# Moving the queries of three expert blocks and the attention units in the order of a decoder step

## The reference

```
q = (xt @ w_pq).reshape(PEER_BLOCK, PEER_HEADS, 2, D_HALF)
s = jnp.einsum('thcd,hckd->thck', q, sub_keys).astype(jnp.float32)
s1, i1 = lax.top_k(s[:, :, 0], PEER_TOPK)
s2, i2 = lax.top_k(s[:, :, 1], PEER_TOPK)
...
top, sel = lax.top_k(cand, PEER_TOPK)
idx = jnp.take_along_axis(cidx, sel, axis=-1)
gate = jax.nn.softmax(top, axis=-1)
h = jnp.einsum('td,thkd->thk', xt, u_tab[idx]).astype(jnp.float32)
a = (jax.nn.gelu(h, approximate=False) * gate).astype(xt.dtype)
return jnp.einsum('thk,thkd->td', a, v_tab[idx])
```

## Time and profile before

| | us |
|---|---|
| median of 3 runs | 1735.94 |
| lowest and highest | 1732.04, 1736.52 |
| the profiled execution, its own time | 1738.4 |
| its span, first to last instruction | 1736.6 |
| PE, DVE, ACT, POOL busy | 1307.0, 1171.6, 811.9, 665.7 |
| DMA queue of the gathers | 604.28 MB, 84.8% of the span of 16 engines |

### The profile page before, as it was taken

How to read it: one execution, slowest core, us unless ns; L and a number is a source line. 1 busy time by engine, 2 the same in 40 slices (tenths; PEclk the granted TensorE clock), 3 DMA queues, 4 the chain that set the end, 5 groups by cost and what they waited for, 6 DMA issues and landing times.

```text
span 1736.6 us, 21554 instructions
## 1 busy us (share of the span) xinstructions
PE 1307.0 (75%) x7059; PEld 474.1 (27%) x7059; DVE 1171.6 (67%) x2760; ACT 811.9 (47%) x2335; POOL 665.7 (38%) x583
## 2 busy tenths in 40 slices
PE   7999977797887876667787677777777676766765
PEld 3454532343443321213232111112111111111110
DVE  2444567788667677777776677777766677677664
ACT  1433355776344455445554455455444445444433
POOL 0000134345444444343435454444444444444441
PEclk9999988898999988988878877877888888888866
DMA  9424599999999999999999999999999999999995
GB/s 358 154 108 154 222 351 402 357 397 377 421 421 421 419 395 420 399 405 399 402 393 379 423 421 421 421 422 421 421 420 421 420 416 422 422 421 420 421 421 209
DMA packets 97745, 656.30 MB, mean 378 GB/s; under 512 B 12432, under 2 KB 17168, under 8 KB 20816
## 3 DMA queue, kind: packets, MB, share of 16 engines
q0 software_dynamic: 83056, 604.28, 84.8%
q1 hardware_dynamic: 14576, 50.64, 7.7%
HBM read 651.66 MB, written 4.19 MB: 378 GB/s over the span
## 4 chain that ended last, share of the span: by engine, by line
DMA 44%; PE 25%; DVE 12%; ACT 10%; issue 7%; POOL 1%; ACTq 0%; SPq 0%; DVEq 0%; POOLq 0%
DMA R<-in_peer_uv,R 43%; PE ps L1933 9%; PE ps L1478 6%; DVE R L1416 4%; PE ps L1737 3%; PE ps L1455 2%; ACT L881 2%; ACT R L890 2%; ACT R L885 1%; ACT R L881 1%; ACT L797 1%; PE ps L1463 1%; DVE R L1246 1%; DVE R L1249 1%; DVE R L1247 1%
## 5 line engine op out<-in xcount | busy, mean ns | idle before, releaser
L1933 PE MATMUL ps<-R 64*64 64x512 f32 x4608 | 751.4, 734 | 394.5 <-ACT R L890 393.2
L612 POOL DMA_INDIRECT R<-in_peer_uv,R x576 | 663.7, 1152 | 973.3 <-PE ps L1933 767.6
L1416 DVE CUSTOM_DVE_ANT_0 R<-R 128x1024 f32<-128x1024 f32 x576 | 700.1, 1224 | 392.1 <-DMA R<-in_peer_uv,R 388.0
L881 ACT ACTIVATE R<-R 128x1 f32<-128x1 f32 x576 | 115.9, 201 | 616.9 <-DVE R L1416 615.3
L1933 PEld LDWEIGHTS ps<-R 64*64 64x64 f32 x4608 | 138.6, 151 | 752.3 <-ACT R L890 653.9
L1737 PE MATMUL ps<-A,R 128*128 128x256 f32 (+1 forms) x640 | 224.7, 478 | 0.7 <-ACT R L773 0.7
L890 ACT ACTIVATE R<-R 128x64 f32<-128x64 f32 x576 | 200.4, 348 | 53.2 <-ACT R L885 0.4
L885 ACT ACTIVATE R<-R 128x1 f32<-128x1 f32 x576 | 169.8, 295 | 20.9
L1737 PEld LDWEIGHTS ps<-A,R 128*128 128x128 f32 (+1 forms) x640 | 94.8, 200 | 264.3 <-issue 261.6
L1478 PE MATMUL ps<-A,R 128*128 128x512 f32 (+1 forms) x256 | 102.8, 554 | 0.0
L1455 PE MATMUL ps<-R 128*128 128x256 f32 (+2 forms) x384 | 89.7, 387 | 1.2 <-DVE R L1315 0.7
(11 more groups left out here) (271 smaller groups left out, 882.2 us busy)
## 6 DMA issues: line engine op xcount, KB each, us to landing
R<-in_peer_uv,R POOLq DMA_INDIRECT x576, 16.2
A<-in_w_pq SPq DMA_DIRECT2D x8, 1024.0 KB, 10.0
A<-in_w_in SPq DMA_DIRECT2D x3, 2048.0 KB, 22.3
R<-in_w_out SPq DMA_DIRECT2D x5, 1024.0 KB, 9.0
R<-in_w_out SPq DMA_DIRECT2D x1, 3072.0 KB, 10.2
R<-in_w_mkv SPq DMA_DIRECT2D x2, 1024.0 KB, 9.3
R<-in_x_promptT SPq DMA_DIRECT2D x4, 512.0 KB, 8.3
x_res<-in_x_prompt SPq DMA_DIRECT2D x4, 512.0 KB, 11.2
```

The lines of the kernel that those rows point to most:

```text
L612: pool.indirect_dma_start(slots[slot_of[g]], None, I["peer_uv"][:, :], bass.IndirectOffsetOnAxis(ap=idx[:, b % 4, k:k + 1], axis=0)).then_ ...
L881: act.activation(hgelu[:, b % 2, col], hdot[:, b % 2, col], ACT.Gelu).then_inc(gelu_ready, 1)
L1416: dve.tensor_tensor_reduce(u, u, xn(t), 1.0, 0.0, ALU.mult, ALU.add, hdot[:, b % 2, k:k + 1]).then_inc(u_used, 1)
L1933: ins = pe.matmul(bank(2 * (t % 2) + q)[rows], diag[tokens, g % DIAGS, :], v_rows[slot_of[g]][tokens, c * 512:(c + 1) * 512], start=first, ...
```

## The change

Block 1's chain is written into the first experts of the loop: the products at g = 0 and 1, the transposes at 3, scores at 5, the copies at 3, 5 and 7, the top 16 at 8 and 9, best pairs at 10, the list at 11, gates at 13. Tile 1's norm moves from ahead of the loop to behind expert 0, and its preparation, cross attention and expert norm each by one expert. `query_at` gets eight more for blocks 2 and 3, so their lists stand at g = 28 and 44 where they stood at 20 and 36; blocks 4 and 12 had these eight before. The units start at 21, 30, 37, 44, 51 and 58 where they started at 22, 29, 36, 43, 50 and 57. The second output piece also waits for the last tile's norm.

```
-        PREP_AT = {1: -1, 2: 122, 3: 204, 4: 236}
-        QUERY_AT = {1: 5, 2: 134, 3: 212, 4: 244}
-        CROSS_AT = {1: 8, 2: 138, 3: 216, 4: 248}
-        FFN_AT = {1: 28, 2: 158, 3: 237, 4: 16 * 23 + 2}
-        UNIT_AT = (22, 29, 36, 43, 50, 57)
+        PREP_AT = {1: 0, 2: 122, 3: 204, 4: 236}
+        QUERY_AT = {1: 6, 2: 134, 3: 212, 4: 244}
+        CROSS_AT = {1: 9, 2: 138, 3: 216, 4: 248}
+        FFN_AT = {1: 29, 2: 158, 3: 237, 4: 16 * 23 + 2}
+        UNIT_AT = (21, 30, 37, 44, 51, 58)
...
-            return (s - 2) * TOPK + (8 if s in (4, 12) else 0)
+            return (s - 2) * TOPK + (8 if s in (2, 3, 4, 12) else 0)
...
 ScalarE, ahead of the loop and in it
-            prep(1, 0)
-            queries_out(1)
-            queriesT_out(1)
-            scores_out(1)
...
+                    if g == 3:
+                        queries_out(1)
+                    if g == 5:
+                        queriesT_out(1)
+                    if g == 7:
+                        scores_out(1)
+                    if g == 13:
+                        gates(1, 1)
...
 VectorE, behind the dot product of g
+                    if g in (8, 9):
+                        top_keys(1, g - 8)
+                    if g == 10:
+                        best_pairs(1)
+                    if g == 11:
+                        experts_of(1, 1)
+                    if g == 14:
+                        finish_gates(1, 1)
...
 TensorE
-            q_mm(1)
-            q_T(1)
-            scores(1)
...
-                pe.wait_ge(n_T, t)
+                pe.wait_ge(n_T, TILES - 1 if n == 1 else t)
...
+                    if g in (0, 1):
+                        q_mm(1, 8 * g, 8 * g + 8)
+                    if g == 3:
+                        q_T(1)
+                    if g == 5:
+                        scores(1)
```

More of the change, by code:

```diff
@@ L411, in held_by @@
             return max((e for e in range(g) if slot_of[e] == slot_of[g]), default=None)
-        PREP_AT = {1: -1, 2: 122, 3: 204, 4: 236}
-        QUERY_AT = {1: 5, 2: 134, 3: 212, 4: 244}
-        CROSS_AT = {1: 8, 2: 138, 3: 216, 4: 248}
-        FFN_AT = {1: 28, 2: 158, 3: 237, 4: 16 * 23 + 2}
-        UNIT_AT = (22, 29, 36, 43, 50, 57)
+        PREP_AT = {1: 0, 2: 122, 3: 204, 4: 236}
[3 more added lines that the diff above has]
+        UNIT_AT = (21, 30, 37, 44, 51, 58)
         OUT_AT = (75, 79, 83, 89, 93, 97, 103, 107, 111, 117, 121, 125)
         def query_at(s):
-            return (s - 2) * TOPK + (8 if s in (4, 12) else 0)
+            return (s - 2) * TOPK + (8 if s in (2, 3, 4, 12) else 0)
         def query_steps(g):
-            return [(s, g - query_at(s)) for s in range(BLOCKS) if 0 <= g - query_at(s) < 2 * TOPK]
+            return [(s, g - query_at(s)) for s in range(2, BLOCKS) if 0 <= g - query_at(s) < 2 * TOPK]
         def units():
@@ L904, in _ @@
                     g = b * TOPK + k
+                    if g == 3:
[6 more added lines that the diff above has]
+                        gates(1, 1)
                     for n, step in query_steps(g):
-                        if step == 9 and n > 1:
+                        if step == 9:
                             queries_out(n)
-                        if step == 11 and n > 1:
+                        if step == 11:
                             queriesT_out(n)
-                        if step == 13 and n > 1:
+                        if step == 13:
                             scores_out(n)
@@ L1416, in _ @@
                     dve.tensor_tensor_reduce(u, u, xn(t), 1.0, 0.0, ALU.mult, ALU.add, hdot[:, b % 2, k:k + 1]).then_inc(u_used, 1)
+                    if g in (8, 9):
[6 more added lines that the diff above has]
+                        finish_gates(1, 1)
                     for n, step in query_steps(g):
-                        if n == 1 and step in (16, 17):
-                            top_keys(1, step - 16)
-                        if n > 1 and step in (14, 15):
+                        if step in (14, 15):
                             top_keys(n, step - 14)
@@ L1960, in _ @@
                     expert(b, k)
+                    if g in (0, 1):
[4 more added lines that the diff above has]
+                        scores(1)
                     for n, step in query_steps(g):
-                        if n > 1 and step < KD:
+                        if step < KD:
                             w = len(heads_of(n))
                             q_mm(n, w * step, w * step + w)
-                        if n > 1 and step == 9:
+                        if step == 9:
                             q_T(n)
-                        if n > 1 and step == 11:
+                        if step == 11:
                             scores(n)
```

## The result

The changed kernel takes 1741.17 us, median of 10 runs (1737.73 to 1743.32), against 1734.43 us for the kernel before, median of 10 on the same chip (1730.71 to 1739.95). The ratio is 1.0041 (95% interval 1.0030 to 1.0053): about 7 us slower. The forecast was no change, 1735.8 us. The time lies in the range of 1727 to 1743; the side was wrong. The profiled execution took 1743.32 us, with a span of 1741.5.

A forecast was written before the change was run, and what follows sets the result against it. DMA time below 422 GB/s, about 23 us winnable, was taken as the bound. Won 2.0 + 0.6, lost 15.0 - 12.5 = 2.5: net 0.1 us won, 1735.8 us against the 1735.94 median; 8-in-10 range 1727 to 1743.

The forecast's parts named there:

- the exchange of Parts 2 and 3: Lists of blocks 2 to 4 with the attention units: 15.0 us lost at late lists, 12.5 us won back, net 2.5 lost.
- the front: Loop start up to gather 20, with block 1's work moved behind expert 0: 2.0 us won (bounds 0 and 4).
- the last unit: Stretch 404 to 416 us: last attention unit one expert further from list 4, winning 0.6 of 1.3 us lost.
- Part 1: Block 1's queries behind expert 0: gathers 5, 10, 20 issued near 222.6, 241.2, 268.7 us; 2.0 us gained by gather 20.
- Rival C: Early experts: moved work does not free slots earlier, early dip keeps 6.8 us; 2.0 less gain, 1737.8 us; chance 0.06.
- Part 2: Queries of blocks 2 and 3 eight experts later: lists of blocks 2, 3, 4 lose 3.8, 6.0, 5.2 us, together 15.0.
- 2.4 + (issue - 19.5): Loss in us at a late list, from issue time after the first landing; base is block 12's 2.4 us at 19.5.
- Part 3: Attention units further apart: the 12.5 us lost between 306 and 402 goes, 15.0 replaces it; last unit wins 0.6.
- I let all of it go: The whole 12.5 us lost between 306 and 402 us, from block 3's work falling on units 0 and 1, disappears.
- The six experts of lead cover: Ahead of expert 75: PE's wait of some 3 us for the first output piece's weights is covered by six experts' lead.
- Rival B: Slower: first top-16 of blocks 2, 3 and 4 each waits 2.63 us for its score copy; 6.2 more, 1742.0 us; chance 0.22.
- Rival A: Faster: late lists are cheap, each cluster loses 1.7 us less, front wins 2 more; 1728.7 us; chance 0.30.

## Why the prediction was wrong

Two terms of the sum failed. The first is the exchange of Parts 2 and 3, 2.5 us lost with lists and units moved together: in the timed runs the two late lists alone cost 6.1 us and the units alone nothing. The second is what was to be won, 2.0 us by the front and 0.6 by the last unit: the whole change takes 7.1, so with front and units the lists' 6.1 became 1.0 more (not told from nothing) and not 2.6 less. How the gap divides between the two terms is not shown, as single prices did not add up in this kernel.

With two traces of each kernel, the time is split by the starts at 24, 64, 80 and 575. Up to 24 the changed kernel is 0.4 us behind (means of -0.3 and 1.2 against 0.0 and 0.0), from 24 to 64 3.0 behind, from 64 to 80 1.4, and behind 80 2.7: 7.5 in all, for 7.1 timed. The forecast had -2.0, +2.5, -0.6 and 0.

**Part 1, up to gather 20: right.** Gather 5 went out at 222.66 (forecast 222.6), 10 at 240.83 (241.2) for the same releaser as before, was used at 246.94 (246.8), and 20 went out at 268.97 (268.7). Counted from dot product 0, dot product 20 came 2.3 and 3.3 us earlier than in the first trace of before, 1.0 and 2.0 than in the second. Rival C is out.

**Part 1, its last step: failed.** "I take 2.0 (bounds 0 and 4) as the gain by gather 20" was carried to the end of the sum, and by dot product 24 nothing of it is left. (At 36 the changed kernel is 2.8 and 2.6 us ahead again, but there block 3's work is moved too; the kernel with only the lists late is 0.9 ahead.) I had written that the cross attention's exponentials "have the block's gate exponential beside them" and priced the issue of gather 20 by it, but not the experts behind. The rows show two pairs of table loads (one to the exponential, one back) within 8.5 us (257.13 to 265.65), TensorE late with experts 14 and 15, and ScalarE then in front of expert 17 waiting for TensorE, 4.01 and 5.03 us. With the old front the same copy at the same expert waits 2.13 and 2.12 us (both lists late, block 2 late), so the rest comes with the new front. The forecast counted instructions on each engine and did not ask what block 2's products stand behind. The gate exponential is weakly supported as a part of the lost gain (2.2 us by the ratios, 0.7 by the medians); the copy's own wait is not, as removing it didn't change the time. VectorE's top 16 of block 2, now at experts 22 and 23, can be about 1 us of it: between dot products 20 and 24 the two kernels with the old front and this list late lose 1.0 and 1.1 us, the changed one 2.0 and 4.5. Two traces of the kernel before differ there by 1.2, so this part is not shown either.

**Part 2: the sum right, its make-up in part.** 15.4 us lost at the three lists for 15.0: 3.0, 6.8 and 5.6 for 3.8, 6.0 and 5.2. Gathers 32, 48 and 64 were released by the list, as forecast. But much of block 3's loss (4.3 of 6.8) comes before gather 48, at gathers 42 and 43, which waited 4.84 and 6.01 us for slots; and gather 32's wait for the list is 1.99 us because gather 30 had already waited 7.60 for the cross attention's projection, 3.24 in the kernel before. The measure "2.4 + (issue - 19.5)" priced lateness of the list, and hit a sum that has slots in it too. With only the lists moved, the same waits for the list are 7.36 and 7.47. The sum came out right by luck in part.

**Part 3: first half near in the traces of the changed kernel, not in the timed runs of its parts; second half wrong.** The exchange of 12.5 us for 15.0 was to cost 2.5, and from 24 to 64 the traces have 3.0. With only the lists moved, one trace has 4.7 us more there than the first of before and 5.7 more than the second, and 6.1 timed. "I let all of it go" did happen: with block 3's list late the kernels win 1.7 to 4.7 us between dot products 24 and 36. The price comes between 36 and 44, 4.5 to 9.6 us, where block 3's late scores, top 16 and best pairs meet the second and third units. The forecast had a wait for these scores (1.7; 1.81 and 3.17 in the changed kernel) but started the price of the list at block 12, where no unit stands. In this stretch the units' new places or the front seem to take some of it back. Which of the two is open: the new front has no time with the old places of the units, as in that order (with the lists at 24 and 36) the engines wait for each other without end. The 0.6 that the last unit was to win did not come. By rates 402 to 420 loses 1.3 us in both kernels; by starts, 64 to 80 is 1.4 us slower in the changed one, and the kernel with only the units moved loses 3.1 there, so this belongs to the units' new places. Gathers 70 and 71 waited 4.35 and 2.39 us for slots. TensorE waited 1.66 us for the first output piece's weights, within the 3 I gave, and gather 82 then 5.78 us for its slot, 3.35 in the kernel before and 8.73 with the units alone. "The six experts of lead cover" was too easily said; a part is made up by expert 88 in the first trace and not in the second.

**The rest, 2.7 us behind expert 80,** has no instruction that differs and lies within what traces with one order differ by. It stays open whether it is a cost.

**Rival B** named 1742.0 us and was nearest in time, but not by its mechanism alone. It wanted 2.63 us of wait at the top 16 of experts 22, 38 and 54; the waits are 0, 1.81 and 0.73, in the second execution 0, 3.17 and 0.94. That is 2.5 and 4.1 us in place of 7.9, and 1.7 was in the forecast. **Rival A** fell: the early lists of the kernel before were worth their place. The list at four experts ahead that I measured the others by (block 12) was in a part of the loop without attention units; I had seen the difference at block 4 and put it down to the list being 1.4 us later.

**The two rules of the Trainium skill.** The Trainium skill ("DMA: Bandwidth & Descriptors", section "Anatomy of one DMA") would have had a gather in use 4.4 us after issue, an estimate from its figures; here gather 10 was in use after 6.1 (240.83 to 246.94) and 20 after 6.3 (268.97 to 275.28). The Trainium skill ("ScalarE: Activation LUTs", section "What ACT_TABLE_LOAD costs") has 2.66 us for a switch; the rows have 1.28, with the exponential 0.02 us behind the load (257.13 to 258.43). By that rule of the Trainium skill the norm behind expert 0 would have taken the front's gain at once; gather 10 still went out 2.8 us and gather 20 0.7 us earlier than before. The measurements decide in both.

## What to carry to other kernels

When a piece of work is moved in several in-order streams, list for each of its copies and releases what the producer stands behind at the new place. Two engines can wait for each other in turn, as the copies here did with 4.0 to 5.2 us, and no count of busy time on one engine shows it. Nor does the wait by itself give a price: one of 4 us was removed here and the time stayed.

A list or a slot that releases a transfer is rarely the only late thing. When one list was made earlier here, gather 64 no longer waited for it, but the next two waited 3.10 and 4.54 us for slots. The prices of single moves (1.9, 4.2, 2.2 us) added up for two edits of one kind and not across kinds.

Before a difference in a stretch with unchanged order is explained, profile the same kernel again: counted from the loop's first, the start of the same instruction differed by up to 3.0 us between two executions of one kernel.

## What was not expected of the hardware

The loop's first dot product started at 216.8 and 212.4 us in two executions of the same kernel, 4.4 of the 7.4 us by which their times differ (1738.40 and 1730.98). In the stretch of 1276 us behind expert 80, with the same order in all kernels, the 14 profiled executions ranged over 9.2 us (0.7%); behind expert 88, where the units' effect has mostly passed, over 6.9 us. The ten timed executions of the kernel before range over 9.2 us as a whole.
